# Moving the short-convolution products into the state scan of a two-block transformer kernel, and reordering its first and last transfers

## The reference

```
z, xbc, dt_raw, sc_b, sc_c, sc_x = split(n @ w_in)      # 1536, 2560, 24, 512, 512, 512 columns
xbc  = silu(causal_dwconv(xbc, conv_ssd_w) + conv_ssd_b)
y    = ssd_scan(xs, dt, A, B, C) + d_skip * xs           # 24 heads of 64, 4 groups, chunks of 128
y    = rmsnorm_per_group(y * silu(z))
y_sc = sc_b * causal_dwconv(sc_c * sc_x, conv_sc_w)      # three taps
h    = h + concat([y, y_sc]) @ w_out
```

## Time and profile before

| | |
|---|---|
| device time | 1691.21 us, median of 3 runs (1690.76 to 1693.2) |
| the profiled execution | 1692.43 us, span 1689.7 us |
| PE busy | 1498.5 us, 89% of the span |
| DVE, ACT, POOL busy | 1107.9, 786.9, 95.0 us |
| mean granted TensorE clock | 0.934 of full speed |

### The profile page before, as it was taken

The page is one execution under the profiler, slowest core; times in us unless marked ns, Lnnn a source line. Parts: engine busy times, 40 slices in busy tenths (PEclk is TensorE's granted clock), DMA queues, the critical chain, the costliest instruction groups (busy, mean ns, idle before and its releaser), DMA issues.

```text
span 1689.7 us, 28578 instructions
## 1 busy us (share of the span) xinstructions
PE 1498.5 (89%) x9356; PEld 1338.2 (79%) x9356; DVE 1107.9 (66%) x2308; ACT 786.9 (47%) x1252; POOL 95.0 (6%) x113
## 2 busy tenths in 40 slices
PE   4998865999959898797999988888799999999996
PEld 4985654998959896576999988888789998888885
DVE  3797354555546744754389999888555556777774
ACT  4643444444445643144456554444344444454542
POOL 0010000000010046400000000000000000000000
PEclk9986777999969998797999999999999999999998
DMA  6440221455523453034445544555675757777753
GB/s 252 152 143 19 77 73 50 162 185 187 186 75 113 162 173 100 0 126 161 162 163 173 176 157 167 186 190 183 201 228 185 240 185 231 246 239 245 242 193 112
DMA packets 102962, 274.45 MB, mean 162 GB/s; under 512 B 8048, under 2 KB 40944, under 8 KB 102272
## 3 DMA queue, kind: packets, MB, share of 16 engines
q1 hardware_dynamic: 63504, 231.76, 40.9%
q10 hardware_dynamic: 39120, 39.98, 7.0%
q0 software_dynamic: 288, 2.10, 0.3%
HBM read 254.93 MB, written 18.87 MB: 162 GB/s over the span
## 4 chain that ended last, share of the span: by engine, by line
PE 72%; DVE 16%; ACT 5%; issue 3%; DMA 1%; POOL 1%; DVEq 1%; ACTq 1%; SPq 0%; POOLq 0%
PE Y L1506 37%; PE AO L1506 31%; DVE wl L813 3%; PE M L1506 2%; ACT wh L394 2%; DVE hots L1278 2%; DVE CV L868 2%; DVE hots L1277 1%; DVE xl L828 1%; DMA raw<-in_stream 1%; PE M L1570 1%; DVE eqs L1252 1%; ACT xh L421 1%; DVE NAT L1257 1%; DVE eqs L1246 1%
## 5 line engine op out<-in xcount | busy, mean ns | idle before, releaser
L813 DVE TENSOR_TENSOR wl<-raw,wh 128x1024 fp32r<-128x1024 f32 x440 | 541.5, 1233 | 359.8 <-ACT wh L394 359.7
L1506 PE MATMUL AO<-xh,wh 128*128 128x256 f32 (+1 forms) x1824 | 526.4, 289 | 32.1 <-ACT hid L689 13.4
L394 ACT CAST wh<-raw 128x1024 fp32r<-128x1024 f32 x440 | 459.4, 1044 | 173.0 <-PE Y L1506 123.7
L1506 PE MATMUL AO<-xl,wh 128*128 128x256 f32 (+1 forms) x1824 | 522.2, 286 | 0.0
L1506 PE MATMUL AO<-xh,wl 128*128 128x256 f32 (+1 forms) x1824 | 521.9, 286 | 0.0
L1506 PEld LDWEIGHTS AO<-xh,wh 128*128 128x128 f32 x1824 | 353.0, 194 | 38.0 <-issue 13.4
L1506 PEld LDWEIGHTS AO<-xl,wh 128*128 128x128 f32 x1824 | 351.7, 193 | 2.6
L1506 PEld LDWEIGHTS AO<-xh,wl 128*128 128x128 f32 x1824 | 353.0, 194 | 0.0
L1506 PE MATMUL Y<-wh,peer_ah 128*128 128x512 f32 x512 | 200.0, 391 | 2.1 <-DVE peer_al L1300 2.1
L1506 PE MATMUL Y<-wh,peer_al 128*128 128x512 f32 x512 | 199.7, 390 | 0.0
L1506 PE MATMUL Y<-wl,peer_ah 128*128 128x512 f32 x512 | 199.2, 389 | 0.0
(11 more groups left out here) (283 smaller groups left out, 1830.0 us busy)
## 6 DMA issues: line engine op xcount, KB each, us to landing
raw<-in_stream SPq DMA_DIRECT2D x440, 512.0 KB, 3.3
gate_spill<-gstage ACTq DMA_DIRECT2D x32, 512.0 KB, 3.5
gates<-gate_spill ACTq DMA_DIRECT2D x8, 2048.0 KB, 14.9
rowg<-in_post ACTq DMA_DIRECT2D x3, 512.0 KB, 16.8
X<-in_x SPq DMA_DIRECT2D x1, 1024.0 KB, 5.1
memx<-in_mem ACTq DMA_DIRECT2D x1, 1024.0 KB, 12.8
keys<-in_keys POOLq DMA_DIRECT2D x1, 1024.0 KB, 8.0
h_spill<-X POOLq DMA_DIRECT2D x1, 1024.0 KB, 7.4
```

Of the source, the lines that this page charges most:

```text
L394: nc.scalar.copy(wh[:, s, :], raw[:, s, :]).then_inc(split_hi, 1)
L813: nc.vector.tensor_tensor(wl[:, s, :], raw[:, s, :], wh[:, s, :].bitcast(F32), ALU.subtract)\
L1506: return nc.tensor.matmul(o, a, b, start=start, stop=stop)
```

## The change

1. The stream is fetched in the order xbc, z, sc (`SC_ORDER` permutes the 12 sc blocks: sc_c and sc_x of tile 0, of tile 1, and so on, then sc_b).
2. The 12 sc products leave their stage and stand in the scan: `sc_wide(n)`, one after each of the steps k = 0 to 6 (n = k + 3), the others ahead of step 0 and between the chunks. Their evacuations and splits stand in ACT's and DVE's scan loops (`sc_out`, `sc_split`). seg now has one bank of AO (it stood one step ahead of y in PE's order, and now stands behind it), since the other serves the sc products with a piece of Y.
3. The short convolution goes from POOL to DVE (`sc_taps`, `sc_gate`), between the steps. POOL's wide products (`spread_xdd`, `spread_xdt`, `skip`) stand ahead of the steps, and can run from the z stage on.
4. The decay products and exponentials stand inside the xbc stage.
5. Scan tiles get other places, so that xh and xl live through the scan.
6. First transfers: X in two halves, the four raw blocks, then colp, all on SP; memory, rows and gains are issued on SP between later blocks; ACT issues only `gain`. The first quarter is normed before the first split, and splits 1 to 3 stand behind the fourth quarter.
7. Last transfers: `fin_x` and `fin_g` go to SP ahead of the end, and the last two blocks are multiplied for tokens 0 to 127 first, then for the rest.

```diff
-                  ("mlp", 2 * FF_CHUNKS), ("xbc", XBC_T), ("sc", 3 * SC_T), ("z", 12), ("wout2", 16),
+                  ("mlp", 2 * FF_CHUNKS), ("xbc", XBC_T), ("z", 12), ("sc", 3 * SC_T), ("wout2", 16),
...
+SC_ORDER = (4, 8, 5, 9, 6, 10, 7, 11, 0, 1, 2, 3)
+SC_LEAD = 3
+SC_TAPS_AT = (0, 2, 4, 6)
+SC_GATE_AT = (9, 10, 11, 12)
...
-            sp.dma_start(X[:, :, :], x).then_inc(x_in, 16)
+            sp.dma_start(X[:, 0, :], x[:, 0, :]).then_inc(x_in[0], 16)
+            sp.dma_start(X[:, 1, :], x[:, 1, :]).then_inc(x_in[1], 16)
             for s in range(SLOTS):
                 sp.dma_start(raw[:, s, :], stream[s]).then_inc(landed[s], 16)
+            sp.dma_start(colp[:, :], cols).then_inc(par_in, 16)
...
+            sp.wait_ge(spilled, 16)
+            sp.wait_ge(hid_lo, FF_CHUNKS + PAIRED + 28)
+            sp.dma_start(fin_x[:, :, :], h2_spill).then_inc(fin_in, 16)
+            sp.dma_start(fin_g[:, :], post_gains[3].partition_broadcast(P)).then_inc(fin_in, 16)
...
+            def sc_out(n):
+
+                act.wait_ge(w_used, STREAM["sc"] + n + 1)
+                nc.scalar.copy(SCX[:, SC_ORDER[n], :], sc_bank(n)[:, 0:TM]).then_inc(a_free, 1)
+                split(STREAM["sc"] + 4, n)
...
+            sc_out(0)
+            sc_out(1)
+            decays(0)
+            sc_out(2)
+            for k in range(16):
+                if k < 15:
+                    decays(k + 1)
+                if k + SC_LEAD < 10:
+                    sc_out(k + SC_LEAD)
...
+            for k in range(16):
+                c, s = divmod(k, 8)
+                dve.wait_ge(seg_exp, k + 1)
+                if k >= 2:
+                    dve.wait_ge(y_prod, k - 1)
+                nc.vector.tensor_tensor(MM[:, k % 2, :, :], EE[:, k % 2, :, :],
+                                        CBM[:, s // 2, :][:, None, :].to_broadcast([P, 3, P]), ALU.mult)\
+                    .then_inc(seg_m, 1)
+                if s % 2:
+                    from_state(c, s // 2)
+                if k + SC_LEAD < 10:
+                    sc_split(k + SC_LEAD)
+                if k in SC_TAPS_AT:
+                    sc_taps(SC_TAPS_AT.index(k))
...
+            for k in range(16):
+                c, s = divmod(k, 8)
+                pe.wait_ge(seg_m, k + 1)
...
+                ins.then_inc(y_prod, 1)
+                if k < 15:
+                    seg(k + 1)
+                if s % 2 == 0:
+                    from_state(c, s // 2)
+                if k + SC_LEAD < 10:
+                    sc_wide(k + SC_LEAD)
...
-            pe.wait_ge(y_add, 4)
+            pe.wait_ge(a_free, A_BASE["sc"] + 12)
+            pe.wait_ge(y_add, 3)
```

More of the change, by code:

```diff
@@ L366, in fetch @@
                         sp.dma_start(raw[:, s, :], stream[place(i, s)]).then_inc(landed[s], 16)
-            fetch((1, (P0 + HALF) // SLOTS), 0, lambda i, s: i * SLOTS + s)
+            fetch((6, STREAM["z"] // SLOTS), 0, lambda i, s: i * SLOTS + s)
+            for n in range(24):
+                b = STREAM["z"] + n
+                sp.wait_ge(split_lo, b - 3)
+                held = STREAM["z"] + (12 + n if n < 12 else SC_ORDER[n - 12])
+                sp.dma_start(raw[:, b % SLOTS, :], stream[held]).then_inc(landed[b % SLOTS], 16)
+            fetch((STREAM["wout2"] // SLOTS, (P0 + HALF) // SLOTS), 0, lambda i, s: i * SLOTS + s)
             fetch((0, (AHEAD - HALF) // SLOTS), P0 + HALF, lambda i, s: i * 8 + (P0 + HALF + 2 * s))
@@ L378, in _ @@
             step = Steps(act, act_step)
[L379 to L385, removed]
+            act.dma_start(gain[:, :], gain_cols).then_inc(gain_in, 16)
             def split(b0, j, i=0):
@@ L604, in _, with xbc_groups @@
                 split(STREAM["xbc"] + 4, j)
[L605 to L611, removed]
+            def xbc_groups(first, last):
+                with act.Fori(first, last) as i:
+                    for j in range(4):
+                        evac("xbc", j, XB[:, i * 4 + j, 3:], TM, i=i)
+                        split(STREAM["xbc"] + 4, j, i)
+                    act.wait_ge(xconv, i * 16)
+                    nc.scalar.activation(XS[:, bass.ds(i * 4 - 4, 4), :], XS[:, bass.ds(i * 4 - 4, 4), :], ACT.Silu)\
+                        .then_inc(xsilu, 1)
+            xbc_groups(1, 3)
+            act.wait_ge(ac_prod, 1)
+            nc.scalar.activation(exs[:, 0:96], M[:, 1, 0:96], ACT.Exp).then_inc(ac_exp, 1)
+            nc.scalar.activation(exs[0:META, 96:120], M[0:META, 1, 96:120], ACT.Exp).then_inc(ac_exp, 1)
+            xbc_groups(3, XBC_T // 4)
             act.wait_ge(xconv, 4 * XBC_T)
             nc.scalar.activation(XS[:, XBC_T - 4:, :], XS[:, XBC_T - 4:, :], ACT.Silu).then_inc(xsilu, 1)
[L615 to L618, removed]
             turned = turned_tiles()
@@ L654, in squares @@
                                          accum_out=stat[:, 24 + g:25 + g]).then_inc(grp_ss, 1)
[L656 to L665, removed]
+            sc_out(0)
[7 more added lines that the diff above has]
+                    sc_out(k + SC_LEAD)
+                if k == 7:
+                    sc_out(10)
+                    sc_out(11)
+                if k in SC_GATE_AT:
+                    sc_high(SC_GATE_AT.index(k))
+                if k == 13:
+                    squares(0)
             squares(1)
@@ L843, in _ @@
             nc.vector.memset(UP[:, :, 0:CONV_W - 1], 0.0).then_inc(conv_pad, 1)
-            for j in range(SLOTS):
+            dve.wait_ge(gain_in, 16)
+            norm_part(0, 0, 0)
+            split(0, 0)
+            for k, q in ((0, 1), (1, 0), (1, 1)):
+                norm_part(0, k, q)
+            for j in range(1, SLOTS):
                 split(0, j)
-            dve.wait_ge(par_in, 32)
-            norm(0)
+            dve.wait_ge(par_in, 16)
             dve.wait_ge(thin_hi, 1)
@@ L1088, in conv4, with xbc_groups @@
                                                            op0=ALU.mult, op1=ALU.add).then_inc(xconv, 1)
[L1090 to L1104, removed]
+            def xbc_groups(first, last):
+                with dve.Fori(first, last) as i:
+                    for j in range(4):
+                        split(STREAM["xbc"] + 4, j, i)
+                    dve.wait_ge(a_free, i * 4 + (A_BASE["xbc"] + 4))
+                    conv4(i)
+            xbc_groups(0, 3)
             dve.wait_ge(ac_exp, 2)
@@ L1109, in _ @@
             nc.vector.tensor_tensor(exs[:, 48:72], exs[:, 48:72], dtz[:, 2, 24:48], ALU.mult).then_inc(xdd_w, 1)
+            xbc_groups(3, XBC_T // 4)
+            nc.vector.memset(SP[:, :, 0:2], 0.0).then_inc(sc_pad, 1)
+            for j in range(12):
+                split(STREAM["z"] + 4, j)
             def heads(t, o=0):
@@ L1128, in group_norm, with masked @@
                         op0=ALU.mult, op1=ALU.mult).then_inc(grp_y, 1)
-            for c in range(TT):
+            def masked(c):
                 dve.wait_ge(cb_prod, c + 1)
@@ new lines, in add_skip, with gate @@
+            def add_skip(c):
+                dve.wait_ge(y_add, 2 * c + 1)
+                dve.wait_ge(xd_done, c + 1)
+                nc.vector.tensor_tensor(YO[c][:, :], YO[c][:, :], XT[:, c + 1, :], ALU.add).then_inc(y_add, 1)
+            def gate(c):
+                dve.wait_ge(y_add, 2 * c + 2)
+                dve.wait_ge(z_out, 3)
+                nc.vector.tensor_tensor(YO[c][:, :], YO[c][:, :], Z[:, c, :], ALU.mult).then_inc(y_gate, 1)
+            first_state(0)
+            first_state(1)
@@ L1464, in group_norm @@
                 inverse_root(stat[:, 28:32], stat[:, 24:28], GW, grp_rstd)
+            pool.wait_ge(xdd_w, 2)
+            pool.wait_ge(tr_out, 3)
+            spread_xdd(0)
             decay_inputs(0)
             decay_inputs(1)
+            pool.wait_ge(tr_out, 7)
             spread_xdt(0)
-            for k in range(2, 4):
-                decay_inputs(k)
-            pool.wait_ge(st_prod, SSD_G)
             spread_xdd(1)
@@ L1717, in _, with xbc_groups @@
                  KT * FOX_H, SSD_H).then_inc(dt_prod, 1)
-            with pe.Fori(0, XBC_T // 4) as i:
-                for j in range(4):
-                    wide("xbc", j, xh, xl, TM, i)
-            with pe.Fori(0, SC_T * 3 // 4) as i:
-                for j in range(4):
-                    wide("sc", j, xh, xl, TM, i)
+            def xbc_groups(first, last):
+                with pe.Fori(first, last) as i:
+                    for j in range(4):
+                        wide("xbc", j, xh, xl, TM, i)
+            xbc_groups(0, 2)
+            pe.wait_ge(dt_a, 2)
+            a1, a2, a0 = dtz[:, 3, 24:48], dtz[:, 3, 48:72], dtz[0:META, 3, 0:24]
+            mm(M[:, 1, 0:24], upper[:, :], a1, True, True)
+            mm(M[:, 1, 24:48], upper[:, :], a2, True, True)
+            mm(M[:, 1, 48:72], later[:, :], a1, True, True)
+            mm(M[:, 1, 72:96], ones[:, :], a1, True, True)
+            mm(M[0:META, 1, 96:120], later[0:META, 0:META], a0, True, True).then_inc(ac_prod, 1)
+            xbc_groups(2, XBC_T // 4)
```

(16 more changed lines are left out.)

347 lines of the change are left out of this document (189 added, 158 removed).

## The result

| | before | after |
|---|---|---|
| device time, median | 1691.65 us (1690.76 to 1693.2, 4 runs) | 1720.06 us (1718.39 to 1721.7, 4 runs) |
| the profiled execution | 1692.43 us, span 1689.7 us | 1718.39 us, span 1716.7 us |
| PE, DVE, ACT, POOL busy | 1498.5, 1107.9, 786.9, 95.0 us | 1511.6, 1106.0, 788.0, 68.3 us |
| mean granted clock | 0.934 | 0.931 |

The ratio of the runs is 1.0167, with a 95% interval of 1.0149 to 1.0184. PE has the same number of matmuls (9356) as before, so the 13 us that it is busy longer are not more of them; most of it is the lower clock.

The account below looks back on a forecast made before the run. PE was taken as the bound, busy 89% of the span. z ending 38.0 sooner, scan +77.8, start -8.3 and end -7.5 gave +24.0: 1692.4 becomes 1716.4, as a median 1715 us, range 1699 to 1723.

Parts of the forecast that it names:

- start: Kernel start: earlier transfers and norm let the first wide product begin at 17.1; -8.3 us, bounds -6 to -9.5.
- xbc and z, without the start: Stages before the scan: sc stage and a stall go, small costs are added; z stage ends 38.0 us sooner.
- y(0) to y(7), waits: Scan steps 0 to 6: PE waits for MM, 4 x 5.2 and 3 x 3.4, 31.0 us.
- y(0) to y(7), PE's work and clock: Scan steps 0 to 6: PE's own work at full clock 33.0 us, plus 2.5 us for each gap's ramp.
- end: Kernel end: gain's and residual's transfer hidden, at most 8.6 us behind PE's end where 15.9 stood; -7.5 us.
- The clock's 25.5: Whole scan: low clock after nine gaps, 2.5 us each, plus 3 in steps 8 to 14; bounds 12 and 32.
- the ring's 3: Scan steps 8 to 14, a ring of y, seg, EE, MM: half clock for two or three steps, 3 us.
- the copy behind the last Silu: z stage: the turn of the third z block needs a copy standing behind the last Silu; 2.1 us added.
- The step on which the prediction stood: Scan: MM(k+1) stands behind a split waiting for the sc product, so PE idles 3.4 or 5.2 us after each.
- the clock stays up: Rival, scan: gaps do not lower the clock; scan 120.1 us, time 1689.5 us; chance 0.10.
- the clock stays down throughout: Rival, whole scan: bursts too short to raise the clock; up to 1759 us, 1724 to 1740 likelier; chance 0.08.
- the products fill the waits: Rival, scan: some MM(k+1) gets ahead of the split, PE never kept by DVE; 1647 us; chance 0.06.

Follow-up runs that it names:

- e1_mm_first: Changed kernel with one place in DVE's order moved: MM(k+1) ahead of the split that waits for step k's sc product; 1666.37 us.
- e2_taps_out: Changed kernel with the four groups of taps moved to odd steps, between MM and the split's low half; 1699.65 us.
- e3_fill_gaps: Changed kernel with extra unread products on PE behind the sc products of steps 0 to 6, 11 after even and 7 after odd steps; 1701.61 us.
- e7_fill_ring: As e5_both, with added unread products in steps 8 to 14, one after even and three after odd steps; 1660.95 us.
- e5_both: Changed kernel with both edits of DVE's order: MM(k+1) ahead of the split, taps after odd steps ahead of the split; 1664.55 us.
- e4_ends_only: Kernel before, with only the change's first and last transfers (edits 6 and 7); 1677.29 us, ratio 0.9915.
- the fastest version: As e5_both, with seg(k+1) ahead of y(k) from step 8 on, in two banks of AO; 1657.59 us.

## Why the prediction was right

It said 1715, the measurement is 1720, and both the sign and the way are the forecast's. Of the 5 us, 3.0 are in the terms (the span grew by 27.0, where the sum had 24.0); the rest is that the profiled execution is the fastest of the four, 1.7 under their median, where 1.2 over it had been assumed. Its terms, from the two traces (positions of the scan's parts: z's end 608.9, y(0) 626.1, y(7) 708.7, y(8) 725.8, wout2 755.8):

| term | predicted | measured |
|---|---|---|
| start | -8.3 | -7.2 |
| xbc and z, without the start | -38.0 | -36.3 |
| scan until y(0) | 16.7 | 17.2 |
| y(0) to y(7), waits | 31.0 | 29.2 |
| y(0) to y(7), PE's work and clock | 33.0 + 17.5 | 53.4 |
| y(7) to y(8) | 14.7 + 2.5 | 17.1 |
| y(8) to wout2 | 24.7 + 5.5 | 29.9 |
| scan in all | 145.6 | 146.9 |
| end | -7.5 | -8.1 |

(The clock's 25.5 is laid out here as seven ramps of 2.5 ahead of y(7), one ahead of y(8), and one and the ring's 3 behind.)

*Start.* Right in kind, 1.1 too much. xl of the first quarter ends at 12.4, and the prediction had it at 11.4: the transposes began at 8.8, not at 8, and a handover stood between each two steps. The 6.8 MB that the prediction puts ahead of the third raw slot are not in its row, since 13.4 us at 402 GB/s are 5.4 MB, and the earlier trace rows has 9 in the first two slices, so the clock is not low at the start; the sum uses neither.

*xbc and z.* The stage that went was 36.4 of it, as costed. The forecast stall in the z stage, the copy behind the last Silu, is there: 2.5 for 2.1. A wait of 1.2 for an xbc evacuation answers to the 1.0 of the exponentials. These two are 0.6 of the 1.7 missing; 0.5 were lost between the first product and xbc; the rest I have not placed.

*The gap.* The step on which the prediction stood is shown three ways: in the rows of the chain; by e1_mm_first, which takes the wait away without removing work and gains 53.7; and by e2_taps_out, in which all waits become the short one. The waits were 4.93 and 3.15 in turn, some 0.25 under the forecast; 0.14 of that is MM, which takes 0.55 there, not the 0.69 of the earlier trace rows.

*The clock.* e3_fill_gaps shows it apart from the waits: 18.5 net, 20.1 from y(0) to y(8), where seven ramps of 2.5 (17.5) had been put. That is the term that was sized too small, while the waits were sized 1.8 too large. They partly cancel, and that is luck: the 2.5 for a ramp is a mean over four gaps of the kernel before, and with the gap of 3.15 alone (e2_taps_out) seven ramps cost 7.9 and not 17.5. e7_fill_ring gives 3.6 for the ring of e5_both, where 3 had been put for that of the change.

The Trainium skill ("TensorE: Matmul & The Clock Gate", section "What's actually happening") has the ramp under 1% of a typical span. Steps 0 to 6 alone lost 18.5 of 1720.1 us by it, 1.1%, and the ring of e5_both lost 3.6 more, so this kernel's runs do not agree, if not by much.

*The ends.* e4_ends_only: 14.9 by itself, 15.8 in the sum, 15.3 in the trace. At the very end the way from the add to the scaling took 2.1 (1710.15 to 1712.27) and not the 3.0 of before, which is why 7.8 stand behind PE's end and not 8.6.

*The rivals.* That the clock stays up is refuted by the granted 0.72; e3_fill_gaps, with 1701.6, is that rival for steps 0 to 6 only. That the clock stays down throughout is refuted by 0.77 for the scan. That the products fill the waits did not happen in the change, since DVE's order is fixed, as the prediction said; in e1_mm_first nearly, and in e5_both wholly, it does happen, and the sign turns. The 1647 of that rival was too low: the ring of steps 8 to 14 and the waits between the chunks stay, and with the ring opened 1657.6 remain.

Of the 62.5 us between the change and the fastest version, 53.7 come from the place of one split in DVE's order.

## What to carry to other kernels

When work is moved between the steps of a serial chain, follow in each engine's order what stands ahead of the chain's next operation: a helper operation that waits for the moved work itself (here the split, which waits for the slot that the product frees) turns filler into a wait as long as its whole way. The cure costs nothing: put the chain's operation ahead of it. And price a gap on PE with the clock behind it: seven gaps of 29.2 us in all took 18.5 us more. That price does not carry over to other gaps: seven of 22.0 us in all took 5.6.

## What the runs showed of the hardware

*The clock's price follows neither the sum of the gaps nor the length of the one just over.* From y(0) to y(8) the change waits seven times, 4.93 and 3.15 us in turn, 29.2 of 99.7 us; e2_taps_out waits seven times 3.15, 22.0 of 80.4 us. The shares are close, 29% and 27%, but filling the waits gave back 20.1 us in the one and 7.9 in the other. From 628 to 698 the granted clock is 0.72 and 0.87. And y(2), behind the same wait of 3.15, runs at half speed in the change, at full speed in e2_taps_out (the chains of the two):

```profile
648.38 1.54 PE Y L1588 x6
644.36 0.88 PE Y L1588 x6
```

Whether the longest gap decides or what lies between the gaps was not measured.

*A y behind a wait takes longer at full clock too.* In the chain, where a piece ends when the next begins, y takes 0.88 behind a wait in e1_mm_first, and 0.62 in e5_both, where nothing waits; the granted clock is 1.00 for both. A part of the 0.26 is overlap: in the timeline the same two are 0.88 and 0.78, as a y without a wait begins 0.16 before the product ahead of it has ended (633.38 and 633.54). The 18.5 us of e3_fill_gaps hold none of it, since there too each of the seven takes 0.88. In the table it is in the row of PE's work and clock, up to seven times 0.26, 1.8 us.

*DVE and POOL hold each other up.* The timeline of the change in the z stage, where POOL's wide products lie beside the splits:

```profile
597.87 3.74 POOL L1523 TENSOR_TENSOR XDD<-XT,exs 128x1536 f32<-128x1536 f32 x1
...
600.48 2.22 DVE L854 TENSOR_TENSOR wl<-raw,wh 128x1024 fp32r<-128x1024 f32 x1 [1.49 <-ACT wh L422]
601.76 3.56 POOL L1541 TENSOR_TENSOR XT<-XT,rowp 128x1536 f32<-128x1536 f32 x1
...
603.67 2.73 DVE L854 TENSOR_TENSOR wl<-raw,wh 128x1024 fp32r<-128x1024 f32 x1 [0.97 <-ACT wh L422]
...
606.90 1.23 DVE L854 TENSOR_TENSOR wl<-raw,wh 128x1024 fp32r<-128x1024 f32 x1 [0.50 <-ACT wh L422]
```

A wl takes 1.23 alone and up to 2.73 beside them; the blocks that lie ready hide it here. The times read as if one stood still until the other is through, not as if both went slower: the wl of 600.48 and of 603.67 end 1.09 and 1.08 after POOL's operation does (601.61 and 605.32), and POOL's XT of 601.76 ends 2.62 after the first of them (602.70), as XDD does after the wl before (598.99). In e1_mm_first it reaches the path:

```profile
634.59 1.23 DVE L854 TENSOR_TENSOR wl<-raw,wh 128x1024 fp32r<-128x1024 f32 x1 [2.86 <-ACT wh L422]
634.59 1.92 POOL L1531 TENSOR_TENSOR AU<-dtz,upper 128x384 f32<-128x384 f32 x1 [3.27 <-PE AO L1587]
635.73 1.07 DVE L1171 TENSOR_TENSOR SP<-SCX 128x272 f32<-128x272 f32 x1
```

POOL's AU, 0.82 alone, takes 1.92 beside a wl that still takes 1.23 (the two began together), and the product of the taps takes 1.07 where the change, with POOL idle, has 0.44 (1.00 and 0.36 in the chains). The MM of the earlier trace rows fits in: 0.69 there, with POOL busy for half of the scan, and 0.55 in the gaps of the change, where POOL has nothing to do. Spans on POOL are rough, no run was made for this, and why the two engines hold each other was not tested.
